# Second adaLN gate summed on VectorE in the third stage, five more units of the first expert job loaded ahead

## Chip, cores and metric

One core of one Trainium2 chip. The metric is the device time of one execution in microseconds. One launch computes one layer on 256 tokens, all in float32.

## The reference

```python
mod = silu(c) @ w_ada + b_ada          # c is (1, 2048), w_ada is (2048, 12288)
shift1, scale1, gate1, shift2, scale2, gate2 = split(mod, 6)
h = rms_norm(x, norm1_g) * (1 + scale1) + shift1
p = h @ w_in                           # 4096 columns: conv value, conv gate, SSM input, SSM gate
y = concat(rms_norm(conformer_conv(...)), rms_norm(s5_ssm(...))) @ w_out
x = x + gate1 * y
h = rms_norm(x, norm2_g) * (1 + scale2) + shift2
y = hier_moe(h)                        # top-1 group of 4, top-2 experts of 8; SwiGLU, 512 wide
x = x + gate2 * y
out = rms_norm(x, final_norm_g)
```

Each product with c sums the 2048 rows of a 2048-column part of w_ada, weighted by silu(c). The MoE weights are 32 experts of 12 MB.

## The kernel before

**Weights** come through a ring of 12 slots of 1 MB (128 partitions of 2048 words, line 136). SP issues the loads in one fixed order; unit n waits until TensorE has used up unit n - 12 (`start`, line 442, semaphore `consumed`). Everything else lies in an arena (line 138) whose regions are used several times. The list has four parts:

- 36 units of the first stage (scale1 and shift1 of w_ada, one column block of w_in);
- 92 units of the second stage, in 28 steps. A step ends in one "in" unit of w_in (32 matmuls, line 730) and begins with some units of w_ada for gate1, scale2, shift2 and gate2 (16 units each, 8 matmuls a unit, line 715). `ada_in_step` says how many: 1 or 2 in the first 20 steps, then 4 or 5;
- 16 units of w_out in the third stage (`out_units`, line 797; 16 matmuls each, line 819). `C_ORDER` (line 429) sets their order over 4 column chunks;
- the expert jobs: 48 units each, for 4 experts: 32 of w_gate and w_up (line 927), then 16 of w_down (line 961). Here 8 jobs run. A job has 64 token slots for each expert; gathers (line 899) and the combine (line 981) are matmuls between the weight steps. Job j+1's gate and up steps follow job j's down steps on TensorE.

**The second stage** hides the SSM and the convolution under the in-units. Its side work is tied to slots, two for each step, before and behind the in-unit (`side`, line 750 on TensorE, 1205 on ScalarE): eight "drive" jobs (line 763) feed VectorE's scans (`quad`, lines 1623 to 1650), eight "read" jobs (lines 777, 780) use the states, three "sum" jobs (line 748) sum over channels. VectorE runs four scan blocks, a convolution (lines 1662, 1666), three scan blocks, a convolution, the channel statistics (line 1675 is its reduction) and the eighth scan block. Each convolution needs a product that POOL makes (`z_tiles`, line 1407) from in-units of chunks 1 and 4. POOL also makes the diagonals of the reads (`diagonal`, lines 1377 and 1381) and turns each finished w_ada part into columns (`columns`, from line 1383; its first operation is line 1388), from a row that ScalarE copied (`ada_copy`, line 1190).

**The third stage**: output units, the first residual on VectorE by chunk (lines 1745 and 1747), transposes of x1 (line 517), router logits, routing on VectorE. Then the first gather of tokens (line 899), which starts at what is called S below. gate2 goes to DRAM (ScalarE, line 1251) and comes back broadcast over the partitions, 1 MB, with the final gain, 1 MB (lines 1296 and 1297). The first job's first 12 units are loaded while the router works.

Of the kernel before, what the change touches and what calls it, by code (L numbers as in the profile page):

```python
# [31 lines left out]
P = 128  # L32
# [15 lines left out]
BE = 4  # L48
# [13 lines left out]
A_UNITS, B_UNITS, C_UNITS, D_UNITS = 36, 92, 16, 48  # L62
# [20 lines left out]
def ada_in_step(g):  # L83

    if g < 20:
        return 2 if g % 2 else 1
    return 5 if g in (25, 26) else 4
# [3 lines left out]
PART_END = [next(g for g in range(STEPS_B) if ADA_FIRST[g + 1] >= KD * (n + 1)) for n in range(4)]  # L91

DRIVE_AT = [0, 3, 6, 9, 25, 28, 31, 35]
READ_AT = [5, 9, 13, 17, 31, 35, 38, 58]
SUM_AT = [49, 51, 54]
# [28 lines left out]
def trunk(nc, a, out):  # L125

    ctx = ExitStack()
    with ctx:
# [60 lines left out]
        wpickT = at(90, 2 * KB).rearrange("p (r t) -> p r t", r=2)  # L189
        gate2 = at(98, 8 * KB)  # L190
# [164 lines left out]
        x_again = sem("x_landed_again")  # L355
        out_done = sem("out_chunk_done")
# [65 lines left out]
        for g in range(STEPS_B):  # L422
# [7 lines left out]
            + [(3, q) for q in range(4)]  # L430
        OUT_BANKS = [(0, 1), (4, 5), (2, 3), (0, 1)]

# [4 lines left out]
        def _(sp):  # L437
# [3 lines left out]

            def start(n, dst, src):

                if n >= RING:
                    sp.wait_ge(consumed, n - RING + 1)
                sp.dma_start(dst, src).then_inc(landed[n % RING], 16)
# [18 lines left out]
            for m in range(C_UNITS):  # L465
                n = A_UNITS + B_UNITS + m
# [15 lines left out]
            def job_units(j, e0):  # L482

                for m, (stage, pr, u, x) in enumerate(JOB_ORDER):
                    s = m % RING
                    e = e0 + (2 * pr + x)
                    sp.wait_ge(consumed, j * D_UNITS + (D_BASE + m - RING + 1))
# [5 lines left out]
                    sp.dma_start(ring[:, s, :], src).then_inc(landed[s], 16)  # L493

            with sp.Fori(0, NB) as j:
                job_units(j, j * BE)
            sp.wait_ge(jobs_ready, 1)
            n_jobs = sp.value_load(jobn[0:1, 0:1], min_val=NB, max_val=JOBS)
            with sp.If(n_jobs > NB):
                with sp.Fori(NB, n_jobs) as j:  # L500
                    e0 = sp.value_load(jobi[0:1, bass.ds(j, 1)], min_val=0, max_val=EXP - BE)
                    job_units(j, e0)
# [10 lines left out]
        def _(pe):  # L513
# [208 lines left out]
            def chunk_unit(n, it, u):  # L722

                s = arrived(n)
                for kk in range(4):
                    k = 4 * u + kk
# [60 lines left out]
            for m, (g, kind, i, k) in enumerate(B_LIST):  # L787
                n = A_UNITS + m
                if kind == "in":
                    side(2 * g)  # L790
                    chunk_unit(n, i, k)
                    side(2 * g + 1)
                else:
                    ada_unit(n, i, k)

            def out_units(ms):
                for m in ms:
                    c, q = C_ORDER[m]
                    s = arrived(A_UNITS + B_UNITS + m)  # L800
                    src, k0 = (uT, 4 * q - 8) if q >= 2 else (conv, 4 * q)
                    if m == 0:
                        pe.wait_ge(chunk_stored, 16)
                        pe.wait_ge(ada_copied, 12)
# [46 lines left out]

            out_units([0])
            out_units([1, 2])
            side(58)
            out_units([3, 4])
            channel_sum(3)
            out_units([5, 6, 7])
# [13 lines left out]
            logits(1)  # L871
            out_units([14, 15])
# [31 lines left out]
            def weights(j, m):  # L904

                for x in range(2):
                    s = (m + x) % RING
                    pe.wait_ge(landed[s], j * 64 + 16 * ((D_BASE + m + x) // RING + 1))

            def gate_up(j, i):  # L910
# [10 lines left out]
                weights(j, 2 * i)  # L921
                for kk in range(4):
                    for x in range(2):
                        s = (2 * i + x) % RING
# [3 lines left out]
                                  ring[:, s, kk * N:(kk + 1) * N], start=(k == 0),  # L928
# [21 lines left out]
            def down(j, pr, u):  # L950
# [5 lines left out]
                for n in range(4):  # L956
                    if u == 0 and pr == 1:
                        pe.wait_ge(down_stored, j * 8 + n + 1)
                    for x in range(2):
                        half = slice(64 * x, 64 * x + 64)  # L960
                        last = mm(ps[half, 2 + n, :], hidT[pr][:, u, half],  # L961
                                  ring[:, (m + x) % RING, n * N:(n + 1) * N], start=(u == 0), stop=(u == 3),
# [58 lines left out]
            for i in range(16):  # L1021
# [3 lines left out]
                gate_up(0, i)  # L1025
# [23 lines left out]
        def _(act):  # L1049
# [133 lines left out]
            def ada_copy(n):  # L1183
# [6 lines left out]
                nc.scalar.copy(modrow[:, :], ps[:, 2, :]).then_inc(ada_copied, 1)  # L1190
# [777 lines left out]
```

## Time and profile before

| | us |
|---|---|
| median of 3 runs | 1540.58 (1540.08 to 1542.13) |
| the profiled execution's own time | 1544.64 |
| its span, first to last instruction | 1542.9 |
| TensorE busy in the span | 1440.0 (93%) |
| VectorE busy | 516.6 (33%) |
| mean granted TensorE clock | 0.978 of 2.4 GHz |
| moved by DMA | 565.47 MB |

The span is a little shorter than the time, which has the start and the end of the launch in it. PE is TensorE, DVE VectorE, ACT ScalarE; a q behind the name is an engine's sequencer. A matmul of float32 is recorded as two. A row of a timeline merges neighbouring instructions of the same line; what stands in brackets is how long the engine was idle before them and who released it. Busy shares are of one engine and can't be added.

### The profile page before, as it was taken

Reading aid. Unit: us, or ns where it says so; the run is one execution under the profiler, and the core shown is the slowest. Engines: PE = TensorE matmul, PEld = TensorE weight load, DVE = VectorE, ACT = ScalarE, POOL = GpSimd, SP = SyncE. Lnnn points to the kernel's source line nnn. Section 1 sums busy time; section 2 is a strip of 40 time slices with the busy share of each in tenths; the row PEclk is TensorE's granted clock in tenths of the full one; section 3 lists DMA queues with packets and bytes.
Section 4 is the critical chain, followed back from the end, with each engine's and each line's share of the span. In section 5 each row is a group of like instructions: output and inputs, shape, how many; then the busy total and the mean of one; then the engine's idle time right before and its main releaser. Section 6 shows DMA issues by size and latency. Waiting matters only on the chain.

```text
span 1542.9 us, 18923 instructions
## 1 busy us (share of the span) xinstructions
PE 1440.0 (93%) x7448; PEld 663.8 (43%) x7448; DVE 516.6 (33%) x934; ACT 159.7 (10%) x254; POOL 116.3 (8%) x112
## 2 busy tenths in 40 slices
PE   4989999999999979999999999999999999999967
PEld 2556777665544443333333333343343343343311
DVE  4236989969553041121121121121121111111105
ACT  3140100000411120000000010010010010010001
POOL 1000048012000045000000000000000000000000
PEclk9799999999999989999999999999999999999989
DMA  9999878689958339999999999999999999999991
GB/s 318 384 389 405 314 272 305 246 311 415 399 195 316 123 121 381 420 421 421 422 422 422 422 422 422 421 422 422 423 422 422 423 421 422 422 422 422 422 420 70
DMA packets 111009, 565.47 MB, mean 367 GB/s; under 512 B 10632, under 2 KB 10816, under 8 KB 52656
## 3 DMA queue, kind: packets, MB, share of 16 engines
q1 hardware_dynamic: 108368, 560.02, 90.4%
q10 hardware_dynamic: 2592, 4.78, 1.0%
q8 instruction: 34, 0.56, 0.1%
q14 instruction: 15, 0.12, 0.0%
HBM read 562.62 MB, written 2.13 MB: 366 GB/s over the span
## 4 chain that ended last, share of the span: by engine, by line
PE 55%; DVE 12%; DMA 12%; PEld 8%; issue 8%; PEldq 3%; SPq 1%; ACT 1%; POOL 0%; DVEq 0%; ACTq 0%
PE ps L927 20%; PE ps L961 15%; DMA ring<-in_exp_w_down 10%; PE ps L899 8%; PE ps L981 6%; DVE arena L1666 6%; PEld ps L730 4%; PEld ps L819 2%; PE ps L517 2%; DMA ring<-in_w_ada 1%; PE ps L819 1%; DVE arena L1636 1%; PEldq L823 1%; PEldq L735 1%; PE ps L533 1%
## 5 line engine op out<-in xcount | busy, mean ns | idle before, releaser
L927 PE MATMUL ps<-ring,arena 128*64 128x512 f32 x2048 | 458.3, 594 | 11.7 <-DMA ring<-in_exp_w_up 8.1
L927 PEld LDWEIGHTS ps<-ring,arena 128*64 128x64 f32 x2048 | 154.7, 137 | 288.0 <-issue 286.2
L961 PE MATMUL ps<-ring,arena 128*64 128x512 f32 x1024 | 245.1, 602 | 24.7 <-issue 11.9
L730 PE MATMUL ps<-arena,ring 128*128 128x256 f32 x896 | 200.8, 383 | 0.1
L730 PEld LDWEIGHTS ps<-arena,ring 128*128 128x128 f32 x896 | 168.4, 190 | 42.2 <-issue 20.9
L961 PEld LDWEIGHTS ps<-ring,arena 128*64 128x64 f32 x1024 | 71.9, 138 | 167.3 <-issue 159.0
L1869 DVE TENSOR_TENSOR arena<-arena,ps 128x512 f32<-128x512 f32 x72 | 49.5, 688 | 277.6 <-PE ps L981 262.9
L899 PE MATMUL ps<-arena 128*64 128x256 f32 x1024 | 124.2, 387 | 6.4 <-issue 3.8
L819 PE MATMUL ps<-ring,arena 128*128 128x512 f32 x256 | 111.4, 594 | 1.3 <-ACT arena L1203 1.3
L1843 DVE TENSOR_SCALAR arena<-ps,mod 128x256 f32<-128x256 f32 x64 | 34.8, 544 | 228.8 <-PE ps L899 228.8
L981 PE MATMUL ps<-arena 128*64 128x512 f32 x448 | 106.6, 596 | 2.9 <-issue 1.9
L899 PEld LDWEIGHTS ps<-arena 128*64 128x64 f32 x1024 | 73.6, 139 | 70.0 <-issue 42.5
L1666 DVE SCALAR_TENSOR_TENSOR arena<-arena 128x256 f32<-128x256 f32 x240 | 95.3, 480 | 0.0
L819 PEld LDWEIGHTS ps<-ring,arena 128*128 128x128 f32 x256 | 48.3, 190 | 60.3 <-issue 60.0
L1857 DVE TENSOR_TENSOR arena<-arena,ps 128x512 f32<-128x512 f32 x16 | 11.0, 688 | 178.4 <-PEq L933 177.2
L1850 DVE TENSOR_TENSOR arena<-ps,arena 128x512 f32<-128x512 f32 x64 | 44.3, 692 | 66.4 <-PEq L967 66.4
L1381 POOL TENSOR_SCALAR skip<-ident,vT 128x128 f32<-128x128 f32 x8 | 48.1, 6012 | 224.4 <-PE ps L780 221.9
L1303 ACT ACTIVATE arena<-ps,mod 128x256 f32<-128x256 f32 x64 | 36.1, 563 | 279.5 <-PE ps L899 279.5
L715 PE MATMUL ps<-ring,ccol 128*32 128x512 f32 x512 | 62.8, 612 | 2.3 <-ACT modrow L1190 1.5
L981 PEld LDWEIGHTS ps<-arena 128*64 128x64 f32 x448 | 32.0, 137 | 70.1 <-issue 70.1
L533 PE MATMUL ps<-ring,ccol 128*32 128x512 f32 x256 | 40.5, 756 | 19.3 <-DMA ring<-in_w_ada 19.3
L1314 ACT COPY arena<-ps 128x512 f32<-128x512 f32 x16 | 9.4, 585 | 380.3 <-PE ps L517 380.3
(262 smaller groups left out, 725.8 us busy)
## 6 DMA issues: line engine op xcount, KB each, us to landing
ring<-in_exp_w_gate SPq DMA_DIRECT2D x128, 1024.0 KB, 19.8
ring<-in_exp_w_up SPq DMA_DIRECT2D x128, 1024.0 KB, 18.6
ring<-in_exp_w_down SPq DMA_DIRECT2D x128, 1024.0 KB, 22.5
ring<-in_w_ada SPq DMA_DIRECT2D x96, 1024.0 KB, 14.2
ring<-in_w_in SPq DMA_DIRECT2D x32, 1024.0 KB, 11.5
ring<-in_w_out SPq DMA_DIRECT2D x16, 1024.0 KB, 14.2
arena<-in_x SPq DMA_DIRECT2D x2, 1024.0 KB, 7.3
arena<-in_x SPq DMA_DIRECT2D x1, 2048.0 KB, 10.4
```

Of the source, the lines that this page charges most:

```text
L533: last = mm(ps[32 * j:32 * j + 32, bank, :], ccol[:, k:k + 1].to_broadcast([P, 32]), ring[:, s, j * N:(j + 1) * N], start=(i == 0), stop=( ...
L715: last = mm(ps[32 * j:32 * j + 32, 2, :], ccol[:, k:k + 1].to_broadcast([P, 32]), ring[:, s, j * N:(j + 1) * N], start=(k == 0), stop=(k = ...
L730: last = mm(ps[:, j // 2, (j % 2) * T:(j % 2 + 1) * T], ring[:, s, kk * N + j * P:kk * N + (j + 1) * P], hT[:, k, :], start=(k == 0 and j ...
L819: last = mm(ps[:, OUT_BANKS[c][t], :], src[:, k0 + kk, t * P:(t + 1) * P], ring[:, s, kk * N:(kk + 1) * N], start=first, stop=end, skip_gr ...
L899: last = mm(ps[half, 6 + k % 2, 0:T], x1p[:, t, k, half], pick[:, t, :], start=(t == 0), stop=(t == 1), skip_group_check=True)
L927: last = mm(ps[64 * x:64 * x + 64, stage, :], xT[:, k, slot:slot + SLOTS], ring[:, s, kk * N:(kk + 1) * N], start=(k == 0), stop=(k == KD ...
L961: last = mm(ps[half, 2 + n, :], hidT[pr][:, u, half], ring[:, (m + x) % RING, n * N:(n + 1) * N], start=(u == 0), stop=(u == 3), skip_grou ...
L981: last = mm(ps[64 * x:64 * x + 64, 6 + t, :], wpickT[:, pr, t * P + 64 * x:t * P + 64 * x + 64], yexp[pr][:, n, :], start=(pr == 0), stop= ...
L1381: gp_.tensor_scalar(skip[:, :], ident[:, :], vT[:, 4, q:q + 1], None, ALU.mult).then_inc(skip_ready, 1)
L1666: ins = V.scalar_tensor_tensor(conv[:, c, :], z, cwT[:, c, j:j + 1], conv[:, c, :], ALU.mult, ALU.add)
L1850: V.tensor_tensor(yexp[pr][:, n, :], ps[:, 2 + n, :], gate2[:, n * N:(n + 1) * N], ALU.mult).then_inc(down_stored, 1)
L1869: V.tensor_tensor(acc[:, t, cc], acc[:, t, cc], ps[:, bank, :], ALU.add).then_inc(added, 1)
```

## The change

- The 16 gate2 units leave the second stage (92 -> 76 units) and stand among the output units (16 -> 32), two behind each of output units 5 to 12. `ada_in_step` is now 0, 1, 0, 1, ... for 8 steps, 1 up to step 19, then 4.
- VectorE sums them (`roll`): unit i times silu(c) of row i, plus the previous sum, in place in the ring; the slot comes free with `rolled`. The last sum is over partitions: four matmuls of ones between the logits and output units 14, 15. Its copy, columns and store follow later on ScalarE and POOL.
- Slots of side work are three a step now; the middle one lies inside the in-unit. Their places are chosen anew.
- POOL: columns of part 0 behind the second product, diagonal 7 behind that product, columns of part 3 behind the token constants.
- The first job has 5 units more ahead, in arena regions (`EXTRA`): 2 when the reads are over, 1 after the fourth output chunk, 1 after the last residual, 1 after the logits. Ring slots of all later units shift by 5.
- The broadcasts of gate2 and of the final gain go into two of these regions and wait until the first job has used up the units there (13 and 14 of its units).
- SP's loop runs from the down units of one job to the hidden units (gate, up) of the next; the last job's down units stand behind the loop.

```diff
-A_UNITS, B_UNITS, C_UNITS, D_UNITS = 36, 92, 16, 48
+A_UNITS, B_UNITS, C_UNITS, D_UNITS = 36, 76, 32, 48
...
-DRIVE_AT = [0, 3, 6, 9, 25, 28, 31, 35]
-READ_AT = [5, 9, 13, 17, 31, 35, 38, 58]
-SUM_AT = [49, 51, 54]
+DRIVE_AT = [1, 3, 9, 15, 37, 44, 50, 55]
+READ_AT = [8, 14, 20, 26, 49, 55, 60, 85]
+SUM_AT = [74, 76, 80]
...
+        EXTRA = [at(kb, UNIT) for kb in (106, 98, 48, 82, 4)]
...
+            def slot_free(n):
+                last = n - RING
+                if last in GATE2_AT:
+                    i = GATE2_AT.index(last)
+                    if i < KD - 1:
+                        sp.wait_ge(rolled, i + 2)
+                    else:
+                        sp.wait_ge(gate2_summed, 1)
+                elif last >= 0:
+                    sp.wait_ge(consumed, consumed_by(last))
...
+                    elif first and m < RING + HELD:
+                        signal = extra_landed[m - RING]
+                        if m < RING + 2:
+                            sp.wait_ge(side_done, QUADS)
+                        elif m == RING + 2:
+                            sp.wait_ge(out_done, 4)
+                        elif m == RING + 3:
+                            sp.wait_ge(x1_ready, 2 * 4)
+                        else:
+                            sp.wait_ge(logits_done, 1)
+                    elif first and m < 2 * RING + HELD:
+                        sp.wait_ge(consumed, CONSUMED + m - RING - HELD + 1)
...
+            HIDDEN, DOWN = range(0, 32), range(32, D_UNITS)
+            job_units(0, 0, HIDDEN, True)
+            with sp.Fori(0, NB - 1) as j:
+                job_units(j, j * BE, DOWN)
+                job_units(j + 1, j * BE + BE, HIDDEN)
             sp.wait_ge(jobs_ready, 1)
...
+            e_last = sp.value_load(jobi[0:1, bass.ds(j_last, 1)], min_val=0, max_val=EXP - BE)
+            job_units(j_last, e_last, DOWN)
...
                 for kk in range(4):
+                    if kk == 2:
+                        middle()
...
+            s = arrived(GATE2_AT[KD - 1])
+            pe.wait_ge(rolled, KD)
+            pe.wait_ge(x1_ready, 6)
+            for j in range(4):
+                last = mm(ps[32 * j:32 * j + 32, 3, :], ones[:, 0:32], ring[:, s, j * N:(j + 1) * N], start=True, stop=True)
+            last.then_inc(gate2_summed, 1)
+            pe.drain().then_inc(ada_done, 1)
             out_units([14, 15])
...
+            act.wait_ge(gate_stored, 32)
+            act.wait_ge(consumed, CONSUMED + RING + 2)
+            act.dma_start(gate2, gate_dram[1:2, :].to_broadcast([P, D])).then_inc(gate2_landed, 16)
             store_hidden(0, 0)
...
             for q in range(4):
                 diagonal(q)
             z_tiles(1)
             diagonal(4)
-            columns(0)
             diagonal(5)
             diagonal(6)
+            z_tiles(0)
             diagonal(7)
-            z_tiles(0)
             pool.wait_ge(z_ready, 2)
             gp_.memset(mean_w, 1.0 / CH).then_inc(sum_consts, 1)
+            columns(0)
             columns(1)
...
+                    if i == 0:
+                        V.tensor_scalar(unit, unit, ccol[:, 0:1], None, ALU.mult).then_inc(rolled, 1)
+                    else:
+                        dve.wait_ge(rolled, i)
+                        V.scalar_tensor_tensor(unit, unit, ccol[:, i:i + 1], ring[:, GATE2_AT[i - 1] % RING, :], ALU.mult,
+                                               ALU.add).then_inc(rolled, 1)
...
+            roll(0, 6)
             dve.wait_ge(ab_turned, 1)
...
+            residual(0)
+            roll(6, 10)
+            residual(1)
...
+            roll(10, 13)
+            residual(2)
+            roll(13, KD)
+            residual(3)
```

## Rows read from the trace of the kernel before

**Rows 1.** Page, second part: what the DMA engines moved, in 40 equal slices of the span.

```profile
GB/s 318 384 389 405 314 272 305 246 311 415 399 195 316 123 121 381 420 421 421 422 422 422 422 422 422 421 422 422 423 422 422 423 421 422 422 422 422 422 420 70
```

**Rows 2.** Windows: us, busy PE, PEld, DVE, ACT, POOL, clock, DMA share, GB/s.

```profile
200.00:300.00 100.00, 98.25 (x583) 71.50 (x576) 93.70 (x189) 7.17 (x11) 49.13 (x11) 1.00 0.75 273
...
500.00:525.00 25.00, 24.74 (x65) 11.29 (x64) 3.96 (x6) 6.41 (x12) 0.00 (x0) 1.00 0.38 126
```

**Rows 3.** Chain of waits, down steps of two jobs: start us, us, what.

```profile
756.49 3.65 PE ps L961 x16
...
875.83 3.65 PE ps L961 x16
```

**Rows 4.** Waits of TensorE for expert weights: us in total, times, longest.

```profile
PE ps L961 <- DMA ring<-in_exp_w_down: 8.7, 7, 1.3
...
PE ps L927 <- DMA ring<-in_exp_w_up: 8.1, 7, 1.3
```

**Rows 5.** Timeline of TensorE, second stage: start us, us, engine, line, operation, count, idle.

```profile
128.48 1.06 PE L715 MATMUL ps<-ring,ccol 128*32 128x512 f32 x8 [0.26 <-issue]
129.48 1.15 PE L763 MATMUL ps<-arena 32*128 32x256 f32 x16
...
216.51 1.94 PE L780 MATMUL ps<-arena 128*32 128x256 f32 x32
...
319.31 7.17 PE L730 MATMUL ps<-arena,ring 128*128 128x256 f32 x32
...
384.35 0.67 PE L748 MATMUL ps<-arena 128*128 128x256 f32 x2 [2.23 <-issue]
...
398.08 0.59 PE L748 MATMUL ps<-arena 128*128 128x256 f32 x2
...
410.14 3.64 PE L715 MATMUL ps<-ring,ccol 128*32 128x512 f32 x32
```

**Rows 6.** Timeline of VectorE, second stage.

```profile
130.76 2.29 DVE L1623 TENSOR_TENSOR arena<-ps,arena 128x2048 f32<-128x2048 f32 x1 [8.49 <-PE ps L763]
...
211.41 1.38 DVE L1662 TENSOR_SCALAR arena<-arena 128x256 f32<-128x256 f32 x4 [5.20 <-POOL arena L1411]
...
330.02 2.82 DVE L1662 TENSOR_SCALAR arena<-arena 128x256 f32<-128x256 f32 x4 [13.28 <-POOL arena L1411]
...
389.72 3.74 DVE L1675 TENSOR_REDUCE arena<-arena 128x256 f32<-128x2048 f32 x1 [1.98 <-ACT arena L1216]
```

**Rows 7.** Timeline of POOL, second stage.

```profile
218.58 42.19 POOL L1381 TENSOR_SCALAR skip<-ident,vT 128x128 f32<-128x128 f32 x1 [7.28 <-PE ps L780]
260.74 1.05 POOL L1388 TENSOR_TENSOR modrow<-modrow,own 128x512 f32<-128x512 f32 x1
```

**Rows 8.** Timeline of TensorE, third stage and first job.

```profile
423.02 20.84 PE L819 MATMUL ps<-ring,arena 128*128 128x512 f32 x48 [1.27 <-ACT arena L1203]
...
481.22 0.24 PE L517 MATMUL ps<-ident,arena 32*128 32x32 f32 x1
...
561.66 9.46 PE L899 MATMUL ps<-arena 128*64 128x256 f32 x64 [2.60 <-DVE arena L1831]
570.95 3.60 PE L927 MATMUL ps<-ring,arena 128*64 128x512 f32 x16
...
636.92 3.65 PE L961 MATMUL ps<-ring,arena 128*64 128x512 f32 x16 [0.83 <-DMA ring<-in_exp_w_down]
```

**Rows 9.** Timelines of VectorE and ScalarE, third stage.

```profile
495.55 0.69 DVE L1745 TENSOR_TENSOR arena<-ps,arena 128x512 f32<-128x512 f32 x1 [10.95 <-PEq L823]
...
460.56 0.33 ACTq L1251 DMA_DIRECT2D gate_scratch<-mod  x1
```

**Rows 10.** VectorE by line and shape: count, busy us, mean ns, idle.

```profile
L1650 DVE TENSOR_TENSOR arena<-arena 128x2048 f32<-128x2048 f32 x8 | 18.3, 2293 | 0.3
...
L1647 DVE SCALAR_TENSOR_TENSOR arena<-arena 128x512 f32<-128x512 f32 x16 | 11.1, 692 | 0.5
```

**Rows 11.** Page, last part: DMA issues, KB each, median us to landing.

```profile
ring<-in_exp_w_gate SPq DMA_DIRECT2D x128, 1024.0 KB, 19.8
```

More of the change, by code:

```diff
@@ L355, in trunk @@
         x_again = sem("x_landed_again")
+        extra_landed = [sem(f"first_job_unit_landed_{e}") for e in range(5)]
+        rolled = sem("gate2_units_added")
+        gate2_summed = sem("gate2_sum_read")
         out_done = sem("out_chunk_done")
@@ L430, in trunk, with consumed_by, job_unit @@
             + [(3, q) for q in range(4)]
-        OUT_BANKS = [(0, 1), (4, 5), (2, 3), (0, 1)]
+        C_LIST = []
+        for m in range(16):
+            C_LIST.append(("out", m))
+            if 5 <= m < 13:
+                C_LIST += [("gate2", 2 * (m - 5)), ("gate2", 2 * (m - 5) + 1)]
+        assert len(C_LIST) == C_UNITS
+        C_BASE = A_UNITS + B_UNITS
+        OUT_AT = [C_BASE + C_LIST.index(("out", m)) for m in range(16)]
+        GATE2_AT = [C_BASE + C_LIST.index(("gate2", i)) for i in range(KD)]
+        CONSUMED = C_BASE + 16
+        def consumed_by(n):
+            return n + 1 - sum(x < n for x in GATE2_AT)
+        OUT_BANKS = [(0, 1), (4, 5), (2, 3), (0, 1)]
+        HELD = len(EXTRA)
+        def job_unit(m, first):
+            if first and m < RING:
+                return ring[:, m, :]
+            if first and m < RING + HELD:
+                return EXTRA[m - RING]
+            return ring[:, (m - HELD) % RING, :]
         block = ctx.enter_context(nc.Block())
@@ L464, in _ @@
                     start(n, unit, w_ada[k, :, c0:c0 + D])
-            for m in range(C_UNITS):
-                n = A_UNITS + B_UNITS + m
+            for x, (kind, m) in enumerate(C_LIST):
+                n = C_BASE + x
+                if kind == "gate2":
+                    start(n, ring[:, n % RING, :], w_ada[m, :, 5 * D:6 * D])
+                    continue
                 c, q = C_ORDER[m]
@@ L961, in down @@
                         last = mm(ps[half, 2 + n, :], hidT[pr][:, u, half],
[L962 removed]
+                                  job_unit(m + x, False)[:, n * N:(n + 1) * N], start=(u == 0), stop=(u == 3),
                                   skip_group_check=True)
@@ L1726, in _, with roll, residual @@
                                        ALU.mult).then_inc(ys_ready, 1)
+            def roll(first, last):
+                for i in range(first, last):
+                    n, unit = GATE2_AT[i], ring[:, GATE2_AT[i] % RING, :]
+                    dve.wait_ge(landed[n % RING], 16 * (n // RING + 1))
+                    if i == 0:
+                        V.tensor_scalar(unit, unit, ccol[:, 0:1], None, ALU.mult).then_inc(rolled, 1)
+                    else:
+                        dve.wait_ge(rolled, i)
+                        V.scalar_tensor_tensor(unit, unit, ccol[:, i:i + 1], ring[:, GATE2_AT[i - 1] % RING, :], ALU.mult,
+                                               ALU.add).then_inc(rolled, 1)
+            def residual(c):
+                for t in range(TT):
+                    dve.wait_ge(out_done, c + 1)
+                    link(V.tensor_tensor(gtmp[:, t, :], ps[:, OUT_BANKS[c][t], :], gate1[:, c * N:(c + 1) * N], ALU.mult))
+                    cc = slice(c * N, (c + 1) * N)
+                    V.tensor_tensor(x1[:, t, cc], x1[:, t, cc], gtmp[:, t, :], ALU.add).then_inc(x1_ready, 1)
+                    dve.wait_ge(x1_ready, 2 * c + t + 1)
+            roll(0, 6)
             dve.wait_ge(ab_turned, 1)
```

123 lines of the change are left out of this document (61 added, 62 removed).

## The prediction

> **What bounds the kernel now.** I read the DMA slices first [rows 1]: from about 600 us to the end the rate stands at 421 to 422 GB/s and never moves, while between 425 and 600 us it sinks to 120 to 200. The windows [rows 2] say what fills the second of these. At 500 to 525 us TensorE is busy 24.74 of 25 us and the DMA engines only 0.38 of the time: the ring of 12 units is full and nothing may be loaded. The chain then gives the period of a job [rows 3]: 875.83 - 756.49 = 119.34 us for 48 units of 1 MB, so **one unit costs 2.486 us** of the DMA engines. TensorE waits for those units 8.7 + 8.1 = 16.8 us in seven jobs [rows 4], 2.4 us a job; a job of its own work would take it 119.34 - 2.4 = 116.9 us. So the jobs are bound by DMA, but by 2% only, and moving loads ahead of them can give back at most 16.8 us. What comes before is different: at 200 to 300 us TensorE is busy 98% and VectorE 94%, DMA 75% [rows 2]. That stage is set by TensorE's written order and by VectorE's chain of scans and convolutions together, and the third stage by TensorE alone. The time is therefore (start of the first job, S = 561.66 us [rows 8]) + (jobs, bound by DMA) + (tail), and I price the change on the first two.
>
> **Second stage.** Sixteen units of w_ada leave TensorE's order: 30 units in the first 20 steps become 16, 34 in the last 8 become 32. A unit costs 3.64/4 = 0.91 us [rows 5]. VectorE's chain decides what of it counts.
> - Start: the first drive used to run at 129.48, ahead of the first in-unit; now it stands in its middle. 128.3 + 7.17/2 + 1.1 = 133.0 against 130.6 (an in-unit takes 7.17 us, a drive 1.1 [rows 5]): the four first scan blocks are 2.3 us later. They ran without a gap from 130.76 to 206.2, where VectorE sat idle 5.2 us before the convolution at 211.41, until POOL's product was there [rows 6]. Eight units less before that product, and a 1.1 us wait for ScalarE's copy that no w_ada unit covers any more at step 4, bring it about 6 us earlier, so now the scans end last: 206.2 + 2.3 = 208.5. The convolution starts 2.8 us earlier.
> - Second convolution, at 330.02 after 13.28 us idle, again until POOL's product [rows 6]. Before that product 14 units less (-12.7), one read moved behind it (0.6 + 1.94 us [rows 5], -2.4 with its issue), the wait at step 4 (+1.1) and about 0.5 of new waits for drive banks: -13.5. The scans end 2.8 earlier, at 313.9, below it. So VectorE's idle time is what pays, and the second convolution ends 13.6 us earlier.
> - POOL's last diagonal now stands before the memset that VectorE's sum waits for. The same operation took 42.19 us beside the first convolution and ended 0.6 us after it [rows 7]; I take +0.9. First channel sum: 384.35 -> 371.65, -12.7 [rows 5].
> - TensorE came to the second sum at 398.08, though its input was there at 389.72 + 3.74 = 393.46 [rows 5, 6]. At its new place TensorE is there first: -4.4. Behind it stand 0.5 + 2 in-units, 8 w_ada units, two sums and the copy, 3.6 + 14.3 + 7.3 + 1.2 + 1.3 = 27.7 against 423.02 - 398.08 = 24.9 us: +2.8. The first output unit starts at 423.0 - 14.3.
> - Columns of parts 1 and 2 on POOL now run right behind the second convolution, beside VectorE's centring and scaling. No row of before shows such an operation of VectorE beside an open POOL operation: between 0 and one length each (1.05 us [rows 7]), twice. I take 1.0 in all, the middle.
>
> The Trainium skill (SBUF — State Buffer, "Who interferes with whom") speaks against this part: a VectorE instruction with two SBUF inputs and a GpSimd instruction that reads SBUF exclude each other for a whole instruction, whichever comes first. By it the first of those two costs is certain rather than possible, and the total would be 1 us above mine. The 42.19 us row agrees with it.
>
> **Third stage.** TensorE gets one gate2 sum of four matmuls, 0.9 us by the w_ada unit [rows 5]. ScalarE's issue of the gate2 store comes now between its last permute and the copy of the logits: 0.33 us [rows 9], +0.4. ScalarE's copy of the gate2 row and POOL's columns follow while TensorE runs the last two output units: nothing, and some microseconds if those units did not cover them. VectorE gets 16 adds of 128x2048. No row shows a scalar_tensor_tensor of that size: 2.29 us by the tensor_tensor, 4 x 0.692 = 2.77 us by four of the 512 form [rows 10]; I take 2.33, the size being equal. That is 37 us (44 at the high end) on an engine that is idle in this stage for 10 us and more per output chunk [rows 9]. They are placed in groups: six between the last scaling and the ab copy (14 us in some 22), four between the first two residuals (9.3, at most 11.1, in 495.55 - 481.22 - 2.9 = 11.4 us [rows 8, 9]), three and three in the next two. All fit, the second group barely. **SP's queue** is where it could go wrong: 16 gate2 units stand in order with the output units, each waiting for a ring slot freed by an output unit or by an add. Walking it through at 20.84/3 = 6.95 us an output unit [rows 8], output unit 9 is issued when unit 5 is used up (454), 10 at 461, 11 at 468, 12 at 475, 13 at 482, 14 and 15 by the 10th and 11th add at 481 and 491; TensorE wants them 475, 483, 490, 498, 505, 518 and 525. Each has 20 us or more against 5 to 10 us of flight. The 17 units of the first job are issued by 538 and in before TensorE touches the first at S + 9.3.
> **S moves by** -14.3 + 1.0 + 0.9 + 0.4 = **-12.0 us** (-10.5 to -13.5 with the bounds).
>
> **Jobs.** The first ring slot of the first job comes free when the first gate step ends, 570.95 + 3.45 = S + 12.8 [rows 8], before and after. Then unit 12 was next, now it is unit 17: 5 x 2.486 = -12.4 us. But the broadcasts of gate2 and of the final gain, 1 MB each, used to run at 555 us in idle DMA time; now they wait until the first job has used up the regions and fall into the full stretch: 2 x 2.486 = +5.0. And in the ramp, with the first slots coming in pairs every 7 us and the window shrinking from 17 to 12, I count 0.5 us of idle DMA. Net **-7 us**. TensorE reaches the first down step at S + 74.4, 0.8 us before the weights do now [rows 8], so it runs unhindered through about (7 - 0.8)/2.4 = 2.6 jobs, then DMA sets the pace again, 7 us ahead. Extra lead means about 3 fewer units in flight out of some 8 (19.8 us from issue to landing [rows 11] over 2.486): still enough to keep the engines full. SP now leaves its loop ahead of the last 16 loads and reads a register twice; those 8 units in flight hide some 15 us of that. Should they not, the last job's down weights come later and the tail with them.
>
> **Sum.** -12 - 7 = -19 us. The profiled execution took 1544.64 us around a span of 1542.9, and the runs' median is 1540.58; the profiled one is 4.1 above and the difference carries over: 1540.6 - 19 = **1521.6 us**. About 0.2%, 3.1 us, is what this measurement can tell from no change. Own range of this case: 1517.5 to 1526.
>
> **Rivals.**
> - *Units ahead give nothing* (11%): the lead of the first job is eaten in the ramp or by TensorE, whose own work is 98% of the DMA's. Then only S moves: 1528.6. For it: 2.4 us a job of margin. Against it: 16.8 us in all, more than twice what is asked.
> - *The two broadcasts cost nothing* (10%), because DMA still has gaps when they run: -12 - 12 = 1516.6. For it: the slice of 579 to 617 us has 381 GB/s, not 421 [rows 1]; against it: the full rate right after.
> - *VectorE's chain doesn't move as computed* (12%): one of POOL's products is locked out by the scans or the read order costs waits, and the second convolution gains 7 instead of 13.6: 1528 to 1532.
> - *Slower* (5%): the adds serialize with the output units. A residual stands behind four adds on VectorE, the adds behind their loads, the loads in SP's queue behind output units that wait for TensorE, which waits for the residual. From the point where gate2 unit 8 lands after about 478 us, each microsecond is TensorE's. With all 16 adds uncovered: -19 + 37 = +18, 1559. For it: the second group's 0 to 2 us of slack; against it: those units are asked for at 454.
> - *It does nothing* (2%): the tail or the exit stall of SP gives all of it back, 1540.6.
>
> **Numbers.** The forecast has 60%. Faster by over 0.2%: the first four cases, 0.92 with some of the slow rival's mild forms taken off; within 0.2% 0.03; slower 0.05. The range reaches from the cheap broadcasts to the stuck VectorE chain: 1514 to 1531.
>
> **What would show it.** Right: second convolution at 316 to 317 us, first output unit near 410, first gather near 549.7, DMA slices fuller between 450 and 550, no wait of TensorE for weights in the first two jobs and about 10 us in all, period 119.3 later. Wrong: an idle row of TensorE in the third stage released by VectorE, a gap over 1 us before a residual, DMA below 420 GB/s after 600, or a first down step that waits.

## The result, and the profile after the change

| | before | changed |
|---|---|---|
| median of 5 runs each, one chip | 1542.13 us | 1533.17 us (1531.57 to 1534.6) |
| ratio, 95% interval | | 0.994 [0.9928, 0.9952] |
| profiled execution, its span | 1544.64, 1542.9 | 1533.17, 1531.4 |
| S, start of the first gather | 561.66 | 560.82 |
| last up step starts at S + | 905.81 | 900.31 |
| waits for expert weights | 8.7 + 8.1 us | 5.3 + 4.7 us |

Faster, but by 9 us and not by 19: 1533.2 lies above the range of 1514 to 1531. S, which was to move by 12 us, stood still in the profiled pair.

Timeline of TensorE, second stage of the changed kernel (start us, us, engine, line, operation, count, idle before and releaser), against [rows 5] and the first row of [rows 8]:

```profile
371.90 5.22 PE L784 MATMUL ps<-ring,ccol 128*32 128x512 f32 x32 [11.46 <-ACT modrow L1272]
377.06 7.17 PE L801 MATMUL ps<-arena,ring 128*128 128x256 f32 x32
384.07 0.59 PE L819 MATMUL ps<-arena 128*128 128x256 f32 x2
...
393.13 0.67 PE L819 MATMUL ps<-arena 128*128 128x256 f32 x2 [1.24 <-issue]
...
408.25 0.67 PE L819 MATMUL ps<-arena 128*128 128x256 f32 x2 [0.32 <-issue]
...
421.06 4.53 PE L890 MATMUL ps<-ring,arena 128*128 128x512 f32 x10 [1.27 <-ACT arena L1285]
```

The new row is the first: 11.46 us in which TensorE does nothing, before the first w_ada units of part 2, because ScalarE has not copied part 1's row out of the PSUM bank they write. The wait costs more than its own length: those 32 matmuls take 5.22 us where four units took 3.64 before [rows 5]. The window from 370 to 375 us shows the granted clock behind the wait, 0.50 of 2.4 GHz, the lower level:

```profile
370.00:375.00 5.00, 3.10 (x16) 0.79 (x20) 1.44 (x1) 2.96 (x4) 3.92 (x10) 0.50 0.23 72
```

The first channel sum stands at 384.07, where I forecast 371.65. ScalarE and POOL say why:

```profile
307.53 0.59 ACT L1272 COPY modrow<-ps 128x512 f32<-128x512 f32 x1 [6.68 <-PEq L788]
...
371.26 0.59 ACT L1272 COPY modrow<-ps 128x512 f32<-128x512 f32 x1 [49.70 <-POOL mod L1479]
```

```profile
315.97 2.20 POOL L1496 TENSOR_TENSOR arena<-arena 128x1024 f32<-128x1024 f32 x1 [14.84 <-ACT arena L1285]
321.25 46.39 POOL L1466 TENSOR_SCALAR skip<-ident,vT 128x128 f32<-128x128 f32 x1 [3.08 <-PE ps L851]
367.58 0.20 POOL L1507 MEMSET arena<- 128x128 f32 x1
367.75 1.06 POOL L1473 TENSOR_TENSOR modrow<-modrow,own 128x512 f32<-128x512 f32 x1
368.88 1.99 POOL L1476 TENSOR_TENSOR modrow<-modrow 128x256 f32<-128x256 f32 x4
370.95 0.22 POOL L1479 TENSOR_TENSOR mod<-modrow 128x16 f32<-128x16 f32 x1
```

Part 0's row was ready at 308.1 (307.53 + 0.59), but in POOL's program columns(0) now stands behind diagonal(7), and that operation is held for 46.39 us, until the second convolution ends. The columns come out at 371.2 (370.95 + 0.22), ScalarE overwrites the row at 371.26, TensorE goes on at 371.90. POOL holds ScalarE, ScalarE holds TensorE, and of these three only POOL counts as busy, with an operation that is itself held.

VectorE, both convolutions' first operations and the sum:

```profile
210.41 1.38 DVE L1747 TENSOR_SCALAR arena<-arena 128x256 f32<-128x256 f32 x4
...
318.27 1.38 DVE L1747 TENSOR_SCALAR arena<-arena 128x256 f32<-128x256 f32 x4 [2.63 <-POOL arena L1496]
319.57 47.59 DVE L1751 SCALAR_TENSOR_TENSOR arena<-arena 128x256 f32<-128x256 f32 x120
367.81 3.63 DVE L1760 TENSOR_REDUCE arena<-arena 128x256 f32<-128x2048 f32 x1 [0.66 <-POOL arena L1507]
```

The second convolution did come 11.75 us earlier, from 330.02 [rows 6] to 318.27, against 13.5 us forecast, and the diagonal cost the memset 0.66 us where I had 0.9. So what I priced there was about right; what I did not price took all of it back.

Third stage, windows (us, busy PE, PEld, DVE, ACT, POOL, clock, DMA share, GB/s) and VectorE's adds by line:

```profile
475.00:500.00 25.00, 24.63 (x64) 11.05 (x63) 18.64 (x17) 7.75 (x14) 0.00 (x0) 1.00 1.02 401
500.00:525.00 25.00, 24.74 (x73) 11.75 (x72) 16.00 (x10) 5.19 (x11) 0.00 (x0) 1.00 1.03 410
```

```profile
L1822 DVE SCALAR_TENSOR_TENSOR ring<-ring,ccol 128x2048 f32<-128x2048 f32 x15 | 35.3, 2351 | 1.3
L1819 DVE TENSOR_SCALAR ring<-ring,ccol 128x2048 f32<-128x2048 f32 x1 | 1.3, 1282 | 0.0
```

The DMA engines, at 0.38 between 500 and 525 us before [rows 2], are full now, and TensorE is as busy as it was.

Jobs: the waits, and the first of them in the timeline.

```profile
PE ps L1043 <- DMA ring<-in_exp_w_down: 5.3, 4, 1.3
...
PE ps L1009 <- DMA ring<-in_exp_w_up: 4.7, 4, 1.2
```

```profile
636.21 3.65 PE L1043 MATMUL ps<-ring,arena 128*64 128x512 f32 x16 [0.56 <-issue]
...
753.65 3.65 PE L1043 MATMUL ps<-ring,arena 128*64 128x512 f32 x16 [0.87 <-issue]
...
988.95 3.65 PE L1043 MATMUL ps<-ring,arena 128*64 128x512 f32 x16 [1.32 <-DMA ring<-in_exp_w_down]
```

TensorE waits for no weights until 988.95, S + 428. Left to itself it needs 753.65 - 636.21 = 117.44 us a job against 119.34 by DMA [rows 3].

A second surprise lies where TensorE leaves its loop over the jobs:

```profile
1461.13 3.65 PE L1009 MATMUL ps<-ring,arena 128*64 128x512 f32 x16 [1.25 <-DMA ring<-in_exp_w_up]
1472.44 6.22 PE L1043 MATMUL ps<-ring,arena 128*64 128x512 f32 x16 [7.66 <-issue]
1478.60 0.66 PE L586 MATMUL ps<-ident,arena 128*128 128x128 f32 x4
```

From the start of the last up step to the transposes: 17.47 us. Before, this stretch took 22.28 us (1467.47 to 1489.75), with two stalls of TensorE, 7.96 and 3.53 us, where there is one now (`issue` in the rows marks idle time for which the profile shows no releaser). I had not forecast that at all. The 16 matmuls behind the stall take 6.22 us and not 3.65, for here too TensorE comes back at the lower clock (granted 0.50 from 1470 to 1475 us); of the 4.8 us, 3.8 are stall and 1.0 is slow matmuls. From the transposes to the end it is 52.8 us (53.15 before).

So in the profiled pair: S -0.8, jobs -5.5 (905.81 - 900.31), exit -4.8, the rest -0.4: 11.5 us of span.

### The profile page after: what moved, and what is told of

Same layout as the page of the kernel before. It is cut to its first block, busy times and chain, and to the rows that moved or that the text cites. A ratio compares the mean times of both kernels' runs of the same rounds, so it can differ in the third digit from the quotient of the medians.

```text
span 1531.4 us, 18660 instructions
## 1 busy us (share of the span) xinstructions
PE 1426.3 (93%) x7328; PEld 660.2 (43%) x7328; DVE 554.0 (36%) x950; ACT 160.0 (10%) x254; POOL 158.9 (10%) x112
## 4 chain that ended last, share of the span: by engine, by line
PE 62%; DVE 13%; DMA 8%; issue 6%; PEld 3%; POOL 3%; PEldq 2%; ACT 1%; SPq 1%; DVEq 0%; ACTq 0%; POOLq 0%
PE ps L1009 23%; PE ps L1043 15%; PE ps L977 8%; PE ps L1063 6%; DMA ring<-in_exp_w_down 6%; DVE arena L1751 3%; POOL skip L1466 3%; DVE arena L1721 2%; PEld ps L890 2%; PE ps L586 2%; PE ps L801 2%; DMA ring<-in_w_ada 1%; PEldq L894 1%; DVE arena L1709 1%; DVE arena L1708 1%
## 5 line engine op out<-in xcount | busy, mean ns | idle before, releaser
L1009 PE MATMUL ps<-ring,arena 128*64 128x512 f32 x2008 | 450.7, 593 | 7.4 <-DMA ring<-in_exp_w_up 4.7
L1043 PE MATMUL ps<-ring,arena 128*64 128x512 f32 x1024 | 244.1, 603 | 19.8 <-issue 10.4
L801 PEld LDWEIGHTS ps<-arena,ring 128*128 128x128 f32 x896 | 167.8, 190 | 43.5 <-issue 21.9
L1466 POOL TENSOR_SCALAR skip<-ident,vT 128x128 f32<-128x128 f32 x8 | 97.7, 12218 | 209.5 <-PE ps L851 207.1
L1751 DVE SCALAR_TENSOR_TENSOR arena<-arena 128x256 f32<-128x256 f32 x240 | 95.2, 477 | 0.0
L784 PE MATMUL ps<-ring,ccol 128*32 128x512 f32 x384 | 47.6, 615 | 12.0 <-ACT modrow L1272 11.5
L602 PE MATMUL ps<-ring,ccol 128*32 128x512 f32 x256 | 40.6, 755 | 19.1 <-DMA ring<-in_w_ada 19.0
L586 PEld LDWEIGHTS ps<-ident,arena 128*128 128x128 f32 (+3 forms) x276 | 31.9, 162 | 38.1 <-issue 35.3
## 6 DMA issues: line engine op xcount, KB each, us to landing
ring<-in_w_ada SPq DMA_DIRECT2D x96, 1024.0 KB, 11.6
```

What stands on the lines that cost most here:

```text
L586: return nc.tensor.transpose(dst, src, ident[0:k, 0:k])
L784: last = mm(ps[32 * j:32 * j + 32, 2, :], ccol[:, k:k + 1].to_broadcast([P, 32]), ring[:, s, j * N:(j + 1) * N], start=(k == 0), stop=(k = ...
L801: last = mm(ps[:, j // 2, (j % 2) * T:(j % 2 + 1) * T], ring[:, s, kk * N + j * P:kk * N + (j + 1) * P], hT[:, k, :], start=(k == 0 and j ...
L1009: last = mm(ps[64 * x:64 * x + 64, stage, :], xT[:, k, slot:slot + SLOTS], unit[:, kk * N:(kk + 1) * N], start=(k == 0), stop=(k == KD - 1 ...
L1043: last = mm(ps[half, 2 + n, :], hidT[pr][:, u, half], job_unit(m + x, False)[:, n * N:(n + 1) * N], start=(u == 0), stop=(u == 3), skip_gr ...
L1466: gp_.tensor_scalar(skip[:, :], ident[:, :], vT[:, 4, q:q + 1], None, ALU.mult).then_inc(skip_ready, 1)
```

## The experiments

Theory W: POOL's order is the whole miss; with columns(0) out of the diagonal's shadow the 12 us are there. Rivals: the sixteen adds or the units ahead fall short. Ratios are to the kernel of before run on the same chip; medians of different experiments can come from different chips.

**Columns before the product.** POOL's order in the changed kernel:

```diff
             diagonal(6)
+            columns(0)
             z_tiles(0)
             diagonal(7)
             pool.wait_ge(z_ready, 2)
             gp_.memset(mean_w, 1.0 / CH).then_inc(sum_consts, 1)
-            columns(0)
```

> POOL's columns of part 0 run ahead of the second product and of the last diagonal. Theory A (the columns stood behind a diagonal that POOL can't run beside the second convolution, and TensorE's 11.46 us at the first unit of part 2 came from that alone): that wait falls below 1 us, the second channel statistics start near 371.7 instead of 384.1, S goes from 560.8 to about 549, and the time from 1533.2 to 1521.5 (1520 to 1524). Theory B (TensorE arrives earlier but then meets another limit, the convolution's end, the weights of the fuller queue or the adds on VectorE): the wait moves elsewhere, the time stays over 1527. A cost of both: columns beside the scans, up to 2 us on VectorE.

Measured: 1519.75 us (1517.84 to 1520.13), ratio 0.9854 [0.984, 0.9868]. TensorE's timeline:

```profile
359.29 3.64 PE L784 MATMUL ps<-ring,ccol 128*32 128x512 f32 x32 [0.26 <-issue]
362.86 7.17 PE L801 MATMUL ps<-arena,ring 128*128 128x256 f32 x32
371.12 0.67 PE L819 MATMUL ps<-arena 128*128 128x256 f32 x2 [1.08 <-issue]
...
380.25 0.67 PE L819 MATMUL ps<-arena 128*128 128x256 f32 x2 [1.24 <-issue]
```

The wait is gone, the first sum stands at 371.12 (forecast 371.65) and S at 547.94. The time is even a little under theory A's range. One call moved up by a few lines is worth 13.4 us. The diagonal is still held (47.32 us), but only the memset waits for it, as forecast. W holds. The cost that I had named is there too: eight scans beside the moved columns took 4.52 us (at 306.08) and not 3.11, and the product after them 3.13 us (at 314.55) and not 2.20.

**Columns between product and diagonal.**

```diff
             z_tiles(0)
+            columns(0)
             diagonal(7)
             pool.wait_ge(z_ready, 2)
             gp_.memset(mean_w, 1.0 / CH).then_inc(sum_consts, 1)
-            columns(0)
```

> Columns of part 0 between the second product and the last diagonal, where they start just as the convolution does. Theory A1 (any POOL operation that reads SBUF is shut out as soon as the convolution's operations with two SBUF inputs run back to back): the columns need 3.7 us and have 1.3, so they end only with the convolution near 367.5; TensorE still waits 10 us or more and the time is within 1 us of 1533.2. Theory A2 (as in the row of before at 330.14, where the columns of part 1 ran through beside the first operations of the convolution): they end by 322, the wait is gone, time as with the columns first, 1521 to 1523.

Measured: 1519.69 us, ratio 0.9855 [0.9841, 0.987], S = 548.46: theory A2, 1.3 us under its range, and A1 is out. POOL:

```profile
317.18 1.06 POOL L1473 TENSOR_TENSOR modrow<-modrow,own 128x512 f32<-128x512 f32 x1
318.31 1.99 POOL L1476 TENSOR_TENSOR modrow<-modrow 128x256 f32<-128x256 f32 x4
...
321.05 1.12 POOL L1466 TENSOR_SCALAR skip<-ident,vT 128x128 f32<-128x128 f32 x1
...
352.99 15.68 POOL L1473 TENSOR_TENSOR modrow<-modrow,own 128x512 f32<-128x512 f32 x1 [30.68 <-ACT modrow L1272]
```

and VectorE beside it:

```profile
317.33 2.79 DVE L1747 TENSOR_SCALAR arena<-arena 128x256 f32<-128x256 f32 x4 [2.62 <-POOL arena L1496]
320.05 47.70 DVE L1751 SCALAR_TENSOR_TENSOR arena<-arena 128x256 f32<-128x256 f32 x120
```

At the head of the convolution POOL gets through: its columns and even the diagonal (1.12 us in place of 46.39) run, and VectorE's four tensor_scalars take 2.79 us where they take 1.38 alone. Once the two-input operations run one behind the other, the next POOL operation is held again, 15.68 us, to the convolution's end. So it is not the convolution as a whole that shuts POOL out. Nor is it how far the sequence has come: the diagonal that slips in starts 1.0 us behind its beginning (321.05 and 320.05), the one in the run before, held 47.32 us, 0.75 us behind it (319.83 and 319.08). What the profiles of all fourteen runs have in common is another thing. Each POOL operation that got through beside the second convolution followed another one without a gap, and each that was held for more than 5 us came when POOL had been idle, for 1.9 to 38.9 us. No run changed that alone, so it is a pattern and not a shown cause.

**The adds.** On top of the columns before the product:

```diff
-V.tensor_scalar(unit, unit, ccol[:, 0:1], None, ALU.mult).then_inc(rolled, 1)
+V.tensor_scalar(unit[:, 0:8], unit[:, 0:8], ccol[:, 0:1], None, ALU.mult).then_inc(rolled, 1)
```

and the fifteen others likewise.

> Columns first, and of the 16 adds of the gate2 units only the first 8 of 2048 columns are made (the rest of the sum is left out); loads, waits and order stay. If the 37 us of adds lie wholly beside TensorE's output units: 1519.75 within 1 us. If they hold up a residual, a ring slot or a load: 1 to 5 us less.

Measured: 1518.92 us, ratio 0.9855 [0.984, 0.987], S = 547.50. With the whole adds it was 1519.75 us on another chip and the ratio 0.9854, so the times show no difference. The traces say it more sharply: from VectorE's first scan block to S it is 416.17 us without the adds (547.50 - 131.33) and 416.06 with them (547.94 - 131.88). The 36.6 us of VectorE's work are hidden, and my slower rival had no foothold.

**No units ahead.**

```diff
-        EXTRA = [at(kb, UNIT) for kb in (106, 98, 48, 82, 4)]
+        EXTRA = []
```

> The extra regions hold no unit; the first job has 12 units ahead as before the change, all else stays. If the five units are worth their DMA time (5 x 2.486 us) as long as the weights set the pace: +12.4, 1545.6, TensorE's waits for weights in the jobs up from 10 to 22 us. If TensorE's own work takes over at part of it: +6 to +9, 1539 to 1542. If lead ahead of the jobs gives nothing: 1533.

Measured: 1543.37 us, ratio 1.0011 [1.0002, 1.002], S = 561.23, waits 11.3 + 9.4 us, last up step at S + 911.95. Five units are worth 10.2 us of time, between the first two theories, and 911.95 - 900.31 = 11.6 us of the jobs: 2.33 us each, where DMA's price is 2.486. Against before, the jobs are 911.95 - 905.81 = 6.1 us longer: that is what is left when the units are out. I put it down to the two broadcasts in the full stretch, for which I had 5.0; only one of them is tested by itself, next.

**The final gain after the loops,** so that one broadcast leaves the full stretch:

```diff
             gate_silus(0, 1)
-            act.wait_ge(consumed, CONSUMED + RING + 1)
-            act.dma_start(fgain, a["final_norm_g"].rearrange("(o d) -> o d", o=1).to_broadcast([P, D])).then_inc(gain_landed, 16)
...
+            act.dma_start(fgain, a["final_norm_g"].rearrange("(o d) -> o d", o=1).to_broadcast([P, D])).then_inc(gain_landed, 16)
             store_hidden(j_last, 1)
```

> The broadcast of the final gain, 1 MB, is loaded behind the last job's loads instead of in the first job. If each broadcast moved into the full stretch costs its DMA time: -2.5 us, 1530.7. If it fell into a gap of the ramp: 0, 1533.2. If it then holds up the last job's down weights: +1 to +2.5.

Measured: 1533.58 us, ratio 0.9946 [0.9933, 0.9959], no different from the changed kernel. The two last up steps:

```profile
1454.90 3.65 PE L1009 MATMUL ps<-ring,arena 128*64 128x512 f32 x16 [1.45 <-DMA ring<-in_exp_w_up]
1460.86 5.35 PE L1009 MATMUL ps<-ring,arena 128*64 128x512 f32 x16 [2.30 <-DMA ring<-in_exp_w_up]
```

The load was issued at 1447.28, ahead of both rows, and these two steps wait 3.75 us together, where the last two of the changed kernel wait 1.25: the megabyte was paid there. **One line later,** behind store_hidden(j_last, 1), it comes when the loads are all but done; with it columns(0) before the product, and the memset before diagonal(7):

```diff
             store_hidden(j_last, 1)
+            act.dma_start(fgain, a["final_norm_g"].rearrange("(o d) -> o d", o=1).to_broadcast([P, D])).then_inc(gain_landed, 16)
```

> Columns of part 0 first, the constants' memset ahead of the last diagonal, and the final gain loaded by ScalarE behind its last copy of hidden values, where the last down weights are already on their way. In the run with the gain loaded earlier TensorE's waits for weights began a job later but the last two up steps waited 3.8 us in place of 1.2. Theory A (the broadcast costs its 2.5 us of DMA time in the full stretch, and that run paid it at the end instead): 1519.75 - 2.5 - 0.65 (VectorE's wait for the memset) = 1516.6. Theory B (the broadcast falls into a gap): 1519.1. It beats both kernels in either case.

Measured: 1517.68 us (1515.17 to 1520.8), ratio 0.9847 [0.9831, 0.9863], the lowest median of all; waits 3.6 + 3.5 us, span minus S 967.75. The three other runs with columns(0) moved have 970.36, 970.14 and 969.70, so the broadcast's place is worth 2.0 to 2.6 us, about one unit's 2.486. The 2.1 us between this median and 1519.75 lie inside the scatter of the runs, so the gain is read from the traces and not from the times.

**The exit.** First whether the two stalls of before are chance, by a second profile of the unchanged kernel:

> The kernel before, unchanged, profiled a second time. Its first profile had two idle stretches of TensorE behind the last loop, 7.96 and 3.53 us with two matmuls between them; the changed kernels have one of 7.7. If the second belongs to the program: again about 22.3 us from the start of the last up step to the transposes. If it is chance of that execution: about 17.5 us, and a span 3 to 5 us shorter than 1542.9.

Measured: 1541.95 us, span 1540.2, S = 559.01.

```profile
1464.57 3.65 PE L927 MATMUL ps<-ring,arena 128*64 128x512 f32 x16 [1.13 <-DMA ring<-in_exp_w_up]
1476.23 1.94 PE L961 MATMUL ps<-ring,arena 128*64 128x512 f32 x2 [8.01 <-issue]
1481.75 5.28 PE L961 MATMUL ps<-ring,arena 128*64 128x512 f32 x14 [3.58 <-issue]
1486.96 0.65 PE L517 MATMUL ps<-ident,arena 128*128 128x128 f32 x4
```

Two stalls again: they belong to the program. And S differs by 2.65 us between two executions of one program, while the rest, 981.2 us, is the same in both. The difference is TensorE's clock. Behind the same idle 2.23 us before the first channel sum, the first profile and the second run the same matmuls:

```profile
384.94 6.19 PE L715 MATMUL ps<-ring,ccol 128*32 128x512 f32 x40
```

```profile
384.00 4.50 PE L715 MATMUL ps<-ring,ccol 128*32 128x512 f32 x40
```

The granted clock from 385 to 390 us is 0.66 in the first and 1.00 in the second: 1.7 us. The other 0.9 us are there when the scans start (130.76 and 129.82), behind a first stage whose granted clocks differ too (0.84 and 0.95 from 20 to 40 us).

Then SP's new loop (hidden part of job j + 1 behind the down part of job j) put alone into the kernel of before:

> The kernel before with SP's loop cut as in the change (down units of a job, then hidden units of the next; the last 16 behind the loop), nothing else. If the shorter exit comes from SP leaving its loop earlier: -4 to -5 us, 1537. If it is chance, or belongs to the place of TensorE's code: 1541.4 within 1 us, and the exit as in the kernel before.

Measured: 1543.84 us, ratio 1.0007 [0.9997, 1.0017], stalls of 7.99 and 3.30 us: SP is not it. Then reads that nobody needs, which shift the code behind them, in the kernel of before:

```diff
+            pe.wait_ge(jobs_ready, 1)
+            for _ in range(4):
+                pe.value_load(job_last[0:1, 0:1], min_val=NB - 1, max_val=JOBS - 1)
             with pe.Fori(0, NB - 1) as j:
                 job(j)
```

> The kernel of before, with four reads of a register (of the last job's number) put into TensorE's program ahead of its loop over the jobs: they do nothing but move all code behind them by some eight instructions. Question: before leaves the loop with two stalls (7.96 to 8.01 us, two matmuls, 3.53 to 3.58 us), the changed kernel with one (7.66 to 7.85). Theory P, the place: where the second stall falls hangs on where TensorE's code lies, so it moves to other matmuls, grows, shrinks or is gone. Rival Q, the work: it belongs to what before does there, so it comes again behind the first two matmuls with 3.5 us. Time: 1541 to 1544 by Q, 3 us less where the stall is gone by P.

> As the run with four reads, with twelve: some 24 instructions of shift. P: the second stall stands elsewhere than in the run with four reads, or is gone (then 17.5 us from the last up step's start to the transposes instead of 22.3). Q: 7.9 and 3.5 us, two matmuls between, as before. Reads themselves: under 2 us on TensorE once, and hidden, since it waits for weights some microseconds later anyway.

> The changed kernel with the same four reads ahead of TensorE's loop. P: a second stall of up to 3.5 us may appear in the exit that had only one of 7.7 (time up to 1536.7), or the one stall changes; Q: one stall of 7.6 to 7.9 us as before, 1533.

Measured, one run each: before with four reads 1535.58 us, exit stall 7.53 us and no second one; with twelve 1537.03 us, 7.67 us and no second one; the changed kernel with four reads 1531.32 us, 7.41 us. The reads are more than I had said. The traces count 12 and 36 instructions more, and ahead of the first down step TensorE stands idle 3.46 us with four reads and 8.60 us with twelve, against 0.83 before, not under 2 us. The slack of the DMA-bound jobs hides it: the last up step starts at S + 905.44 and S + 905.38, before at S + 905.81. With four reads, timed:

> The kernel of before with four register reads ahead of TensorE's loop again, now timed. The look at it showed the exit with one stall (7.53 us) and 17.5 us from the last up step's start to the transposes, 4.8 us less than before, and a time of 1535.6, of which the start of the first job (557.69, against 559.01 in the second look at before and 561.66 in the first) is partly chance. If the exit's 4.8 us are real in every execution: ratio to before 0.997, some 1537. If they were an accident of that execution: 1.000.

Measured: 1537.08 us (1535.59 to 1539.58), ratio 0.9971 [0.996, 0.9981].

```profile
1464.88 3.65 PE L927 MATMUL ps<-ring,arena 128*64 128x512 f32 x16 [1.01 <-DMA ring<-in_exp_w_up]
1476.18 6.45 PE L961 MATMUL ps<-ring,arena 128*64 128x512 f32 x16 [7.65 <-issue]
1482.57 0.66 PE L517 MATMUL ps<-ident,arena 128*128 128x128 f32 x4
```

Four reads that nobody needs make the kernel of before 4.5 us faster by the ratio, 4.9 by the medians. The profile's page has a line for the DMA queue that loads instructions; before, then with four reads (packets, MB, share):

```profile
q8 instruction: 34, 0.56, 0.1%
```

```profile
q8 instruction: 33, 0.54, 0.1%
```

One packet of 0.56/34 MB, some 16 KB of code, less. The three profiles with a second stall have 34 packets, those of before with reads 33, those of the changed kind 32. So rival Q is out: the second stall does not belong to the work behind the loop, which is the same in all of them. Theory P, the place of the code, fits every run, and by the packets the stall is a load of code that fell just behind the loop. No run shifts the code without reads and a wait added, so P is the best account and not fully shown. The Trainium skill (Runtime: NRT & Kernel Launch, "Instruction fetch mechanics") has the rule: code comes in blocks of 16 KiB, read ahead in sequence, and a taken branch to a block that isn't held waits for its load. The size of the packets agrees. That the 7.4 to 8.0 us stall, which no run removed, is the jump out of the loop by the same rule, fits it and is not shown.

## Why the prediction was wrong

**The step that failed** is in the second stage: "POOL's last diagonal now stands before the memset that VectorE's sum waits for." I had the held diagonal, by [rows 7], with its release at the convolution's end, and priced it for the memset alone: 0.9 us. Behind the same diagonal stood columns(0), a term that I put at nothing. Later in the same list I even had the columns of parts 1 and 2 "run right behind the second convolution", and asked only whether they would get in VectorE's way. That part 0's stood there as well, and who waits for them, I did not ask: ScalarE's copy of part 1, and through the PSUM bank TensorE's first unit of part 2. Before, columns(0) ran ahead of the diagonal and the product, so the chain had slack. The price: 11.46 us in the trace, 13.4 us in the times (1533.17 - 1519.75), and between the mean S of four runs of either order 561.03 - 548.01 = 13.0, of which the scans' start explains 1.1 (133.11 against 132.03). The wait itself is 11.2 of it (11.46 against 0.26). Behind the wait come slow matmuls at the lower clock, 5.22 to 6.04 us in the four runs for what takes 3.64, +2.0 in the mean; against them stand 0.6 to 1.1 us that TensorE, once early, waits before the first sum. The prediction had no term for the clock.

It was none of my rivals. "VectorE's chain doesn't move as computed" has a time near the one measured (1528 to 1532), but the chain did move.

**Point by point.**
- Start of the scans, +2.3: 132.6 in the mean of the eight runs of the changed kind, 129.85 in that of the six of before's kind: +2.7.
- First convolution 208.5: 210.41. Second 316.5: 318.27. POOL's first product started at 202.81, beside the last scans; that group of eight took 4.98 us, and 3.11 us in other blocks. That is 1.9 us late, and of the kind that I had held possible only for a rival.
- First sum to second, -4.4: 13.73 us before (384.35 to 398.08), 9.13 with the columns moved (371.12 to 380.25), so -4.6. But 1.7 of the 13.73 are the slow clock of that one execution; four of the six profiles of before's kind have 12.04. There the new place is worth 2.9. Second sum to first output unit, 27.7: 380.25 to 408.19, so 27.9. Right. Third stage +1.3: 560.82 - 421.06 = 139.76 against 561.66 - 423.02 = 138.64, so +1.1. Right, adds and SP's queue included.
- The 1.0 us for columns beside VectorE: with the columns moved, part 1's are out at 370.99, before VectorE's centring starts at 372.23, so that cost is nothing. Beside part 2's columns (at 400.39) VectorE's last scaling took 4.53 us, before 3.26, and TensorE did not wait for it. The prediction's remark that by the Trainium skill the total would be 1 us higher needs both costs in full; with the second at its middle it is 0.6. And the 42.19 us of [rows 7] do not simply agree with a lock for one whole instruction: the diagonal was held over about a hundred VectorE operations.
- S, -12.0: the runs with the columns moved have 548.0 in the mean, those of before's kind 559.6: -11.6. Right but for the POOL order; with it +1.4.
- Jobs, -7: -5.5. The terms -12.4 and +5.0 measured -11.6 and +6.1, and the 0.5 us for the ramp are in these; this is the term that was mis-sized. TensorE's own job is 117.44 us, not 116.9, since a wait for weights hides an issue gap of 0.87 us that shows where the weights are there; so it ran free for (988.95 - 636.21)/117.44 = 3.0 jobs behind its first down step and not 2.6. The 10 us of waits came as forecast.
- The tail, for which the sum has no term, held (-0.4); the exit, which I took as fixed, gave 4.8 us.
- One reading of [rows 1] was loose: between 425 and 600 us the rate is not 120 to 200 throughout; one slice has 316. Nothing in the sum rests on it.

The terms close: +1.4 - 5.5 - 4.8 = -8.9 us against 1533.17 - 1542.13 = -8.96. With the columns moved: -11.6 - 5.5 - 4.8 = -21.9 against 1519.75 - 1541.39 = -21.6; my 1521.6 was 1.9 us from that kernel, and that nearness is in part luck: an exit gain that I had not forecast made up for the jobs and for a base, the median of three runs, that was 0.8 us low.

What is open: why POOL gets through at the head of the second convolution in one order and not in another, beyond the pattern above; what the stall of 7.4 to 8.0 us is that every kernel has at the loop's exit; and how the extra 1.1 us of the broadcasts and the missing 0.8 us of the units divide in the ramp.

## What to carry to other kernels

When an operation that will be held for long is moved in an engine's program, list everything behind it on that engine, not only the one semaphore it used to guard, and for each ask who waits for it and through which buffer: here a bank that TensorE wanted again, two engines away. Fill and order such an engine so that the held operation comes last. And when two versions differ by a few microseconds at a loop's exit, compare the stalls marked issue and the packets of the instruction queue before crediting the change: half of this one's gain arose at the exit, and four idle reads gave the kernel of before the same. A stall of TensorE is also to be priced with the slow matmuls behind it: 11.46 us of wait brought 1.6 us more.

## What the runs showed of the hardware that I had not expected

- One stall of 3.3 to 3.6 us behind a loop is there or not with four register reads ahead of the loop; it is worth 0.3% here.
- TensorE's clock behind one and the same idle stretch differs between executions: behind 2.23 us of idleness the granted clock was 0.66 from 385 to 390 us in one and 1.00 in another.
- S varies by up to 4 us between executions of nearly the same code (557.69 to 561.66), and the jobs and tail behind it by next to nothing (981.2 twice). Where a stage's gain is read from single profiles, a mean of several is needed, or the granted clocks of the stretches beside them.
